# Weights of a hybrid decoder trunk loaded in pairs of chunks: 1 MB transfers into a ring of three pairs

## The chip, the core and the metric

The kernel runs on one core of one Trainium2 chip. The metric is device time in microseconds of one execution, median over runs. TensorE (PE in the profile) multiplies, VectorE is DVE, ScalarE is ACT, GpSimd is POOL, and SyncE (SP) does nothing but issue DMA transfers, in order: an issue that waits for a semaphore holds up all issues behind it. The transfers themselves run on 16 DMA engines that all queues share.

## The reference

A batch of 256 tokens of width 2048 goes through two residual layers, all in float32. Cut to what matters:

```python
h = h + even_layer(h, ...)      # layer 0
h = h + odd_layer(h, ...)       # layer 1

def even_layer(h, ...):
    p = rms_norm(h, norm_g) @ w_in          # 2048 x 9232
    # q, k, v: short conv, silu, l2_norm; beta, decay -> gated DeltaNet, 8 heads of 128, chunks of 64
    #   per chunk: solve (I + A) [u, w] = rhs, A strictly lower triangular, then a scan over 4 chunks
    # glu -> depthwise conv of 31 taps -> layer_norm -> silu
    # q_m -> softmax attention into 256 memory tokens, 4 heads of 256
    return concatenate([o_a, o_b, o_m]) @ w_out    # 3072 x 2048

def odd_layer(h, ...):
    p = rms_norm(h, norm_g) @ w_in          # 2048 x 10240
    # stick-breaking attention, 16 heads of 128; memory attention
    return concatenate([o_c, o_m]) @ w_out         # 3072 x 2048
```

The memory tokens are projected once, by a matrix of 2048 x 2048. All weights together are some 230 MB, each read once.

## The kernel before

**Chunks.** Every projection is cut into jobs of 512 columns, and a job into chunks of 256 rows x 512 columns: 512 KB of float32 each, 432 chunks (0 to 431). A job has 8 chunks, those of the output matrices 4. In each chunk TensorE multiplies two k tiles in three products each, of high parts and remainders: `xhi*whi`, `xhi*wlo`, `xlo*whi` (lines 1671 to 1679). With whole jobs that is 12 products of 512 columns or 24 of 256.

**The way of a chunk c.** SyncE loads it into slot `c % 6` of the ring `raw` (`load_chunk`, L725; `RAWS` is 6). ScalarE rounds it into `whi` (`split`, L927), when the chunk has landed and slot `c % 7` of the second ring is free, that is when TensorE is through with chunk c-7. VectorE computes the remainder `wlo = raw - whi` (`rest`, L1284) and counts `s_lo`; with that the `raw` slot is free. The load of chunk c waits for the remainder of chunk c-6. TensorE takes the chunk when its remainder is made (`do_chunk`).

**The order.** `make_plan` writes one list of steps by position (about one position per chunk), and each engine runs its own steps of it in that order. `split(c)` and `rest(c)` stand up to four positions ahead of TensorE's chunk c, and loads 9 ahead. Between the chunks stand all the other steps: DeltaNet, convolution, norms, attention.

**The start.** Chunks 0 to 7 are loaded by lines of their own (`FIRST` is 8), between pieces of x; loads from the plan begin with chunk 8. In the same stretch x is transposed piece by piece: TensorE (L1723), ScalarE (L973) and VectorE (L1330, `xlo`) each do a part, two pieces for each chunk of the first job.

**The block inversion.** For each of two groups g of four DeltaNet heads the triangular matrices are inverted, from 16x16 diagonal blocks up. The blocks go through DRAM, by four transfers in SyncE's queue, which stand at places that the plan gives among the loads:

- inA (L753, `dn_matrices<-hid`, 512 KB) when VectorE has scaled the four matrices;
- inB (L757, `mix<-dn_matrices`, 64 KB) when inA has landed. VectorE then inverts the blocks (`do_inF`, L1441 to L1447, 29 small instructions in a row);
- inC (L765, `dn_block_inverses<-mix`, 64 KB) when that is done;
- inD (L772, `mix<-dn_block_inverses`, 512 KB) when inC has landed. VectorE then turns the matrices (`do_inT`, L1435, two instructions), and after the first TensorE begins the next level (`do_d4x`, L1831).

Of the kernel before, what the change touches and what calls it, by code (L numbers as in the profile page):

```python
# [52 lines left out]
JOBS = []  # L53
# [32 lines left out]
CH0 = []  # L86
# [6 lines left out]
JOB_OF = [j for j in range(len(JOBS)) for _ in range(JOBS[j][3] // 2)]  # L93
# [35 lines left out]
RAWS, RING, AHEAD = 6, 7, 4  # L129
FIRST = 8  # L130
# [189 lines left out]
def prog(nc, x, mem, vecs, w, a_log, dt_bias, out, last_job=len(JOBS)):  # L320
# [4 lines left out]
    with ctx:  # L325
        def sb(name, shape, dt=F32):
            return ctx.enter_context(nc.sbuf_tensor(name, shape, dt))

        def sem(name):
            return ctx.enter_context(nc.semaphore(name))  # L330


        raw = sb("raw", [128, RAWS, 2, 512])
# [106 lines left out]
        s_raw = [sem(f"raw_chunk_loaded{i}") for i in range(RAWS)]  # L440
# [4 lines left out]
        s_lo = sem("chunk_remainders")  # L445
# [272 lines left out]
        def _(sp):  # L718
            def load_chunk(c):
# [3 lines left out]
                if c >= RAWS:  # L723
                    sp.wait_ge(s_lo, c - RAWS + 1)
                sp.dma_start(raw[:, c % RAWS, :, :], w[name][r:r + 256, c0:c0 + 512].rearrange("(k p) n -> p k n", p=128)  # L725
                             ).then_inc(s_raw[c % RAWS], 16)

            sp.dma_start(*vecs(vrow)[0]).then_inc(s_gain, 16)
            for k, loaded in ((0, s_raw0), (1, s_raw[0])):
                sp.dma_start(raw[:, 0, k, :], w["ev_in"][128 * k:128 * k + 128, JOBS[0][2]:JOBS[0][2] + 512]).then_inc(loaded, 16)  # L730
            for step in (("chunk", 1), ("x", 2), ("chunk", 2), ("x", 3), ("chunk", 3), ("chunk", 4), ("x", 4), ("chunk", 5)):
                if step[0] == "chunk":
                    load_chunk(step[1])
                else:
                    c0, c1 = X_PIECES[step[1]]
# [35 lines left out]
                    sp.wait_ge(s_t[1], LEVELS + 1)  # L771
                sp.dma_start(tinv8, rows_t).then_inc(s_inD, 16)  # L772

            steps = {"load": load_chunk, "inZ": do_inZ, "inA": do_inA, "inB": do_inB, "inC": do_inC, "inD": do_inD}
            for st, i in plan:
                if st in steps:
                    steps[st](i)
# [1 line left out]
            for b in range(4):  # L779
                j = last_job - 4 + b  # L780
# [14 lines left out]
        def _(gp):  # L795
# [87 lines left out]
            def do_sbk(_):  # L883
                gp.wait_ge(s_xl, F_H)
                link(nc.gpsimd.memset(mflat[:, 21 * S:24 * S], 1.0))
                keep(beyond[:, 0:128], [[-1, 128]], -1, 1, ALU.is_gt, 0.0)
                keep(beyond[:, 128:384], [[-1, 256]], 127, 1, ALU.is_gt, 0.0)
                keep(valid[:, 0:128], [[1, 128]], 0, -1, ALU.is_gt, 0.0)
                nc.gpsimd.affine_select(out=valid[:, 256:384], in_=valid[:, 256:384], compare_op=ALU.is_gt, fill=0.0,
                                        base=0, pattern=[[1, 128]], channel_multiplier=-1).then_inc(s_sbk, 1)  # L890
# [17 lines left out]
        def _(sc):  # L908
# [7 lines left out]
            def split(c):  # L916

                if c == 0:
                    sc.wait_ge(s_raw0, 16)
                    act(whi[:, 0, 0, :], raw[:, 0, 0, :], ACT.Copy).then_inc(s_hi0, 1)  # L920
                    return
                sc.wait_ge(s_raw[c % RAWS], 16 * (c // RAWS + 1))
                if c >= RING:
                    sc.wait_ge(s_pe, c - RING + 1)
                if c == 2 * RING - 1:
                    sc.wait_ge(s_bap, 1)
                act(whi[:, c % RING, :, :], raw[:, c % RAWS, :, :], ACT.Copy).then_inc(s_hi, 1)  # L927

            def do_half(_):
                sc.wait_ge(s_raw[0], 16)  # L930
                act(whi[:, 0, 1, :], raw[:, 0, 1, :], ACT.Copy).then_inc(s_hi, 1)

            def do_first(_):
                sc.wait_ge(s_vp, 1)
                act(vt[:, 0:16], M[0][:, 0:16], ACT.Copy).then_inc(s_vt, 1)
                sc.wait_ge(s_vt, 1)
# [310 lines left out]
            def do_xload(b):  # L1247
                sc.wait_ge(s_mixa, 8)
                sc.dma_start(hid[:, :, 512 * b:512 * b + 512],
                             x[:, 512 * b:512 * b + 512].rearrange("(t p) d -> p t d", p=128)).then_inc(s_xre, 16)  # L1250

            steps = {"split": split, "evac": do_evac, "xt": do_xt, "mf": do_mf, "rstd": do_rstd,
                     "rrow": do_rrow, "baw": do_baw, "ba": do_ba, "bat": do_bat,
                     "za": do_za, "dnC": do_dnC, "dnS": do_dnS, "dnB": do_dnB, "dnV": do_dnV, "dnG": do_dnG, "d4x": do_d4x,
# [5 lines left out]
            for b in range(2):  # L1260
                c0, c1 = X_PIECES[b]
# [782 lines left out]
```

## Time and profile before

| | before |
|---|---|
| timed runs, us | 1359.11 median of 3 (1358.84 to 1359.45) |
| the profiled execution, us | 1357.89 |
| its span, us | 1356.2 |
| PE busy | 1347.3 us, 99% |
| DVE busy | 891.5 us, 66% |
| ACT busy | 759.4 us, 56% |
| DMA moved | 239.31 MB, mean 176 GB/s |
| loads of chunks | 431 issues of 512 KB, 4.2 to 4.8 us median to landing |

How to read it: the span is the profiled stretch of one execution, and times below are microseconds from its start. Busy time of TensorE is of pipelined products whose ends are modelled. A timeline row has the start, the length, the engine, the line, the operation, out<-in, the shapes and the count of like instructions merged; in brackets stands how long the engine had been idle before it, and what ended that. SPq rows are issues by SyncE's queue: a merged row lasts from its first issue to the end of its last. Such a row doesn't tell when a transfer landed; that stands in the rows of DMA issues, which have the KB each and the median time from issue to landing.

### The profile page before, as it was taken

What the parts mean: (1) busy time and instruction counts of PE and PEld (TensorE: products, weight loads), DVE (VectorE), ACT (ScalarE), POOL (GpSimd) and SP (SyncE); (2) the same over time, 40 slices, a digit from 0 to 9 for tenths busy, and PEclk for the clock granted to TensorE, in tenths of its full rate; (3) what the DMA queues carried; (4) which work ended last, traced back from release to release, by engine and by line L of the source; (5) the groups of instructions that cost most, each with busy time, mean ns of one, the idle gap of its engine ahead of it and who ended that gap; (6) DMA issues with size and microseconds to landing.
All of it is one profiled execution on the core that took longest, in us unless ns stands there. A gap on an engine that the chain in (4) does not pass through costs nothing.

```text
span 1356.2 us, 18328 instructions
## 1 busy us (share of the span) xinstructions
PE 1347.3 (99%) x6925; PEld 1143.4 (84%) x6925; DVE 891.5 (66%) x1337; ACT 759.4 (56%) x1226; POOL 103.4 (8%) x104
## 2 busy tenths in 40 slices
PE   9999999999999999999999999999999999999998
PEld 8998899888888888888888888888888888888887
DVE  5567688899998987645656455655745736556663
ACT  6556634485355567664445546746757657765341
POOL 2000300003100000000002020020100200000000
PEclk9999999999999999999999999999999999999999
DMA  9665554565646755654556564464464654544662
GB/s 315 194 187 170 154 178 139 156 193 148 192 140 202 269 180 172 203 171 140 171 162 197 185 201 131 165 217 156 161 203 134 202 171 154 189 155 139 201 188 77
DMA packets 134512, 239.31 MB, mean 176 GB/s; under 512 B 13936, under 2 KB 19993, under 8 KB 134425
## 3 DMA queue, kind: packets, MB, share of 16 engines
q1 hardware_dynamic: 131705, 233.43, 54.6%
q10 hardware_dynamic: 2720, 4.72, 1.0%
q8 instruction: 55, 0.90, 0.3%
q14 instruction: 32, 0.26, 0.1%
HBM read 234.32 MB, written 3.80 MB: 176 GB/s over the span
## 4 chain that ended last, share of the span: by engine, by line
PE 77%; DVE 3%; issue 0%; POOL 0%; ACT 0%; DVEq 0%; POOLq 0%
PE job L1671 23%; PE job L1673 23%; PE job L1672 23%; PE mixer L1723 3%; DVE cvr L1533 1%; DVE wlo L1284 1%; PE mixer L1939 1%; PE mixer L1959 1%; PE mixer L1977 1%; PE mixer L1990 1%; PE mixer L1831 0%; PE mixer L1976 0%; PE mixer L1991 0%; PE mixer L1812 0%; DVE hid L1509 0%
## 5 line engine op out<-in xcount | busy, mean ns | idle before, releaser
L1284 DVE TENSOR_TENSOR wlo<-raw,whi 128x1024 fp32r<-128x1024 f32 x431 | 529.1, 1249 | 145.6 <-ACT whi L927 145.5
L1671 PE MATMUL job<-whi,xhi 128*128 128x512 f32 x1536 | 615.3, 401 | 0.0
L1673 PE MATMUL job<-whi,xlo 128*128 128x512 f32 x1536 | 600.0, 391 | 0.0
L1672 PE MATMUL job<-wlo,xhi 128*128 128x512 f32 x1536 | 598.3, 390 | 0.0
L927 ACT ACTIVATE whi<-raw 128x1024 fp32r<-128x1024 f32 x431 | 445.6, 1056 | 158.3 <-PE job L1673 114.8
L1673 PEld LDWEIGHTS job<-whi,xlo 128*128 128x128 f32 x1536 | 288.3, 188 | 62.2
L1672 PEld LDWEIGHTS job<-wlo,xhi 128*128 128x128 f32 x1536 | 289.1, 188 | 55.6
L1671 PEld LDWEIGHTS job<-whi,xhi 128*128 128x128 f32 x1536 | 288.7, 188 | 55.2
L1677 PE MATMUL job<-xhi,whi 128*128 128x256 f32 x376 | 108.3, 288 | 0.7 <-DVE wlo L1284 0.7
L1679 PE MATMUL job<-xhi,wlo 128*128 128x256 f32 x376 | 106.4, 283 | 0.0
L1678 PE MATMUL job<-xlo,whi 128*128 128x256 f32 x376 | 106.3, 283 | 0.0
L1533 DVE SCALAR_TENSOR_TENSOR cvr<-cvr,vt 128x255 f32<-128x255 f32 (+14 forms) x240 | 106.0, 498 | 0.2
L1677 PEld LDWEIGHTS job<-xhi,whi 128*128 128x128 f32 x376 | 72.1, 192 | 0.9 <-issue 0.9
L1678 PEld LDWEIGHTS job<-xlo,whi 128*128 128x128 f32 x376 | 72.1, 192 | 0.0
L1679 PEld LDWEIGHTS job<-xhi,wlo 128*128 128x128 f32 x376 | 72.0, 191 | 0.0
L963 ACT ACTIVATE proj<-job,rstd 128x512 f32<-128x512 f32 x68 | 43.0, 688 | 44.6 <-PE job L1673 40.9
L1316 DVE TENSOR_TENSOR hid<-hid,job 128x512 f32<-128x512 f32 x46 | 29.5, 682 | 42.4 <-PE job L1673 42.4
L1630 DVE SCALAR_TENSOR_TENSOR scr<-mixer,scr 128x384 f32<-128x384 f32 x16 | 8.9, 558 | 60.9 <-ACT scr L1235 60.9
L1233 ACT ACTIVATE scr<-mixer 128x384 f32<-128x384 f32 x16 | 7.9, 492 | 60.0 <-PE mixer L1977 60.0
L832 POOL TENSOR_TENSOR ex<-ei,mhalf 128x16 f32<-128x16 f32 x4 | 15.2, 3808 | 305.0 <-DVE ei L1624 305.0
L973 ACT ACTIVATE xhi<-mixer,vt 128x256 fp32r<-128x256 f32 x48 | 20.8, 470 | 29.7 <-PE mixer L1723 29.7
L1723 PE MATMUL mixer<-ident,proj 128*128 128x128 f32 x208 | 35.5, 272 | 1.1 <-DVE mix L1573 0.6
(278 smaller groups left out, 1004.1 us busy)
## 6 DMA issues: line engine op xcount, KB each, us to landing
raw<-in_od_w_in_dram SPq DMA_DIRECT2D x160, 512.0 KB, 4.4
raw<-in_ev_w_in_dram SPq DMA_DIRECT2D x143, 512.0 KB, 4.2
raw<-in_ev_w_out_dram SPq DMA_DIRECT2D x48, 512.0 KB, 4.8
raw<-in_od_w_out_dram SPq DMA_DIRECT2D x48, 512.0 KB, 4.7
raw<-in_w_mem_kv_dram SPq DMA_DIRECT2D x32, 512.0 KB, 4.5
reg<-in_mem_dram ACTq DMA_DIRECT2D x4, 512.0 KB, 5.0
hid<-in_x_dram ACTq DMA_DIRECT2D x4, 512.0 KB, 8.3
hid<-in_x_dram SPq DMA_DIRECT2D x3, 512.0 KB, 8.6
```

The source lines that it names most:

```text
L927: act(whi[:, c % RING, :, :], raw[:, c % RAWS, :, :], ACT.Copy).then_inc(s_hi, 1)
L963: ins = act(dst, pj[j % 2][t][:, :], ACT.Copy, scale=rstd[:, src, t:t + 1])
L1284: vec.tensor_tensor(wlo[:, c % RING, :, :], raw[:, c % RAWS, :, :], whi[:, c % RING, :, :].bitcast(F32), ALU.subtract).then_inc(s_lo, 1)
L1316: ins = vec.tensor_tensor(v, v, pj[j % 2][t][:, :], ALU.add)
L1533: ins = vec.scalar_tensor_tensor(out=c[:, d:], in0=gsrc[:, 0:S - d], scalar=vt[:, col:col + 1], in1=c[:, d:], op0=ALU.mult, op1=ALU.add)
L1671: mm(out_, xh, hi, start=first, stop=False)
L1672: mm(out_, xh, lo, start=False, stop=False)
L1673: return mm(out_, xl, hi, start=False, stop=last)
L1677: mm(out_, hi[:, cols], xhi[:, k, :], start=first and n % 2 == 0, stop=False, skip_group_check=True)
L1678: mm(out_, hi[:, cols], xlo[:, k, :], start=False, stop=False, skip_group_check=True)
L1679: return mm(out_, lo[:, cols], xhi[:, k, :], start=False, stop=last, skip_group_check=True)
L1723: return nc.tensor.transpose(dst, src, ident[:, :])
```

## The change

From chunk 8 on, SyncE loads two chunks, c and c+1 with c even, in one transfer of 1 MB into two neighbouring slots of `raw`. The ring is the same memory, now three pairs. The transfer waits until the remainders of both chunks that held the two slots are made (c-6 and c-5), and it counts on the semaphore of the even slot. ScalarE waits for that one semaphore for either chunk. The step of the odd chunk in the plan issues nothing. Chunks 0 to 7 are loaded as before. The space in `raw`, the bytes and the run of 2 KB from each row of the weights are the same.

```diff
+            def load_pair(c):
+                if c % 2:
+                    return
+                j = JOB_OF[c]
+                name, r0, c0, _, _ = JOBS[j]
+                r = r0 + 256 * (c - CH0[j])
+                sp.wait_ge(s_lo, c + 2 - RAWS)
+                sp.dma_start(raw[:, c % RAWS:c % RAWS + 2, :, :],
+                             w[name][r:r + 512, c0:c0 + 512].rearrange("(a k p) n -> p a k n", p=128, k=2)
+                             ).then_inc(s_raw[c % RAWS], 16)
...
-            steps = {"load": load_chunk, "inZ": do_inZ, "inA": do_inA, "inB": do_inB, "inC": do_inC, "inD": do_inD}
+            steps = {"load": load_pair, "inZ": do_inZ, "inA": do_inA, "inB": do_inB, "inC": do_inC, "inD": do_inD}
...
-                sc.wait_ge(s_raw[c % RAWS], 16 * (c // RAWS + 1))
+                first = c if c < FIRST else c - c % 2
+                sc.wait_ge(s_raw[first % RAWS], 16 * (first // RAWS + 1))
```

The orders of TensorE, VectorE, ScalarE and GpSimd are the same before and after, only lines below the new function are numbered 11 or 12 higher. SyncE's differs. Its queue at the first group's inversion, before: the 37 loads are those of chunks 20 to 56, the three are 57 to 59, the two 60 and 61. `dn_matrices<-hid` is inA, and the next three without `raw` are inB, inC and inD; in brackets are the semaphores that an issue waits for, `chunk_remainders` being `s_lo`.

```order
L725 DMA raw<-in_ev_w_in_dram 128x2x512 [waits chunk_remainders] x37
L753 DMA dn_matrices<-hid 128x8x128 [waits dn_matrices]
L757 DMA mix<-dn_matrices 64x16x16 [waits inv_matrices_stored]
L725 DMA raw<-in_ev_w_in_dram 128x2x512 [waits chunk_remainders] x3
L765 DMA dn_block_inverses<-mix 64x16x16 [waits inv_scratch_cleared,inv_diagonal_blocks_inverted]
L725 DMA raw<-in_ev_w_in_dram 128x2x512 [waits chunk_remainders] x2
L772 DMA mix<-dn_block_inverses 128x8x128 [waits inv_block_inverses_stored]
```

The same place in SyncE's queue now: the 19 loads are the pairs from 20, 21 to 56, 57.

```order
L735 DMA raw<-in_ev_w_in_dram 128x4x512 [waits chunk_remainders] x19
L764 DMA dn_matrices<-hid 128x8x128 [waits dn_matrices]
L768 DMA mix<-dn_matrices 64x16x16 [waits inv_matrices_stored]
L735 DMA raw<-in_ev_w_in_dram 128x4x512 [waits chunk_remainders]
L776 DMA dn_block_inverses<-mix 64x16x16 [waits inv_scratch_cleared,inv_diagonal_blocks_inverted]
L735 DMA raw<-in_ev_w_in_dram 128x4x512 [waits chunk_remainders]
L783 DMA mix<-dn_block_inverses 128x8x128 [waits inv_block_inverses_stored]
```

Chunk 57's load has moved from behind inB to ahead of inA, together with its wait. SyncE's queue at the second group's inversion, before: loads 62 to 107, inA, inB, loads 108 to 110, inC, loads 111 and 112, inD.

```order
L725 DMA raw<-in_ev_w_in_dram 128x2x512 [waits chunk_remainders] x46
L753 DMA dn_matrices<-hid 128x8x128 [waits dn_matrices]
L757 DMA mix<-dn_matrices 64x16x16 [waits inv_matrices_stored]
L725 DMA raw<-in_ev_w_in_dram 128x2x512 [waits chunk_remainders] x3
L765 DMA dn_block_inverses<-mix 64x16x16 [waits inv_block_inverses_loaded,inv_diagonal_blocks_inverted]
L725 DMA raw<-in_ev_w_in_dram 128x2x512 [waits chunk_remainders] x2
L772 DMA mix<-dn_block_inverses 128x8x128 [waits inv_updated1,inv_updated0,inv_block_inverses_stored]
```

And now: pairs up to 106, 107; two pairs, 108, 109 and 110, 111, ahead of inC; pair 112, 113 ahead of inD.

```order
L735 DMA raw<-in_ev_w_in_dram 128x4x512 [waits chunk_remainders] x23
L764 DMA dn_matrices<-hid 128x8x128 [waits dn_matrices]
L768 DMA mix<-dn_matrices 64x16x16 [waits inv_matrices_stored]
L735 DMA raw<-in_ev_w_in_dram 128x4x512 [waits chunk_remainders] x2
L776 DMA dn_block_inverses<-mix 64x16x16 [waits inv_block_inverses_loaded,inv_diagonal_blocks_inverted]
L735 DMA raw<-in_ev_w_in_dram 128x4x512 [waits chunk_remainders]
L783 DMA mix<-dn_block_inverses 128x8x128 [waits inv_updated1,inv_updated0,inv_block_inverses_stored]
```

Chunk 111's load has moved ahead of inC, and chunk 113's ahead of inD.

## Rows read from the trace of the kernel before

**Rows 1.** The page: busy time by engine, and TensorE's granted clock in tenths.

```profile
PE 1347.3 (99%) x6925; PEld 1143.4 (84%) x6925; DVE 891.5 (66%) x1337; ACT 759.4 (56%) x1226; POOL 103.4 (8%) x104
...
PEclk9999999999999999999999999999999999999999
```

**Rows 2.** TensorE's waits: for whom, us in total, times, longest us.

```profile
PE mixer L1723 <- DVE mix L1573: 0.6, 1, 0.6
PE mixer L1723 <- ACT scr L1125: 0.6, 1, 0.6
...
PE mixer L1831 <- POOL reg L862: 0.4, 1, 0.4
```

**Rows 3.** Timeline of the second layer, VectorE from 879 and ScalarE from 883.

```profile
879.57 10.32 DVE L1284 TENSOR_TENSOR wlo<-raw,whi 128x1024 fp32r<-128x1024 f32 x6
...
889.58 0.47 ACT L1225 ACTIVATE cvr<-mixer,qgain 128x256 f32<-128x256 f32 x1 [4.76 <-PE mixer L1723]
```

**Rows 4.** DMA issues at 16.20 (load 8), 22.4 (load 9), 157.1 (56), 163.6 (inB).

```profile
raw<-in_ev_w_in_dram SPq DMA_DIRECT2D x1, 512.0 KB, 9.5
...
raw<-in_ev_w_in_dram SPq DMA_DIRECT2D x1, 512.0 KB, 4.6
...
raw<-in_ev_w_in_dram SPq DMA_DIRECT2D x1, 512.0 KB, 3.7
...
mix<-dn_matrices SPq DMA_DIRECT2D x1, 64.0 KB, 2.9
```

**Rows 5.** Timeline from 16 to 30: SyncE, ScalarE, VectorE, TensorE.

```profile
16.20 6.64 SPq L725 DMA_DIRECT2D raw<-in_ev_w_in_dram  x2
...
25.72 1.06 ACT L927 ACTIVATE whi<-raw 128x1024 fp32r<-128x1024 f32 x1 [1.68 <-DMA raw<-in_ev_w_in_dram]
...
27.96 0.87 DVE L1330 SCALAR_TENSOR_TENSOR xlo<-mixer,vt,xhi 128x256 fp32r<-128x256 f32 x2
...
29.20 0.36 PE L1677 MATMUL job<-xhi,whi 128*128 128x256 f32 x1
```

**Rows 6.** Timeline of SyncE's queue, 160 to 191: inA, inB, inC, inD.

```profile
160.43 0.37 SPq L753 DMA_DIRECT2D dn_matrices<-hid  x1
163.62 0.69 SPq L757 DMA_DIRECT2D mix<-dn_matrices  x1
...
176.05 0.60 SPq L765 DMA_DIRECT2D dn_block_inverses<-mix  x1
...
179.87 0.47 SPq L772 DMA_DIRECT2D mix<-dn_block_inverses  x1
```

**Rows 7.** Timeline of VectorE and TensorE, 162 to 180: remainders, the inversion's first step.

```profile
162.73 1.21 DVE L1284 TENSOR_TENSOR wlo<-raw,whi 128x1024 fp32r<-128x1024 f32 x1
...
169.28 0.16 DVE L1441 TENSOR_SCALAR mix<-mix 64x15 f32<-64x15 f32 x1
...
177.08 1.21 DVE L1284 TENSOR_TENSOR wlo<-raw,whi 128x1024 fp32r<-128x1024 f32 x1
...
179.13 0.28 PE L1677 MATMUL job<-xhi,whi 128*128 128x256 f32 x1
```

**Rows 8.** Timeline at 187: VectorE turns the first matrix, TensorE's next level.

```profile
186.77 0.71 DVE L1435 STREAM_TRANSPOSE mix<-mix 128x512 f32<-128x512 f32 x1 [2.80 <-DMA mix<-dn_block_inverses]
...
187.77 1.06 PE L1831 MATMUL mixer<-mix,reg 128*128 128x128 f32 x8
```

**Rows 9.** Timeline of the second group: inC, inD, VectorE's turn, TensorE's next level.

```profile
347.08 0.59 SPq L765 DMA_DIRECT2D dn_block_inverses<-mix  x1
...
349.82 0.40 SPq L772 DMA_DIRECT2D mix<-dn_block_inverses  x1
...
356.78 0.71 DVE L1435 STREAM_TRANSPOSE mix<-mix 128x512 f32<-128x512 f32 x1 [1.44 <-DMA mix<-dn_block_inverses]
...
357.59 1.13 PE L1831 MATMUL mixer<-mix,reg 128*128 128x128 f32 x8
```

**Rows 10.** Busy time by engine, with granted clock, DMA share and GB/s, 165 to 180.

```profile
165.00:180.00 15.00, 15.00 (x128) 15.00 (x127) 14.04 (x41) 6.63 (x7) 0.00 (x0) 1.00 0.49 122
```

## The prediction

> **What bounds the kernel now.** Read the page first. TensorE is busy 99% of the span, and its granted clock is full in all 40 slices [rows 1]. So only time in which TensorE waits can be won, and every microsecond in which it is made to wait is lost. Next come TensorE's own waits: after the start the longest are 0.6, 0.6 and 0.4 us in total, and none of these is ended by a weight load [rows 2]. The loads are hidden: ScalarE makes a chunk's high part and VectorE its remainder well before TensorE reaches it. What matters is therefore the few places where TensorE starts within a few tenths of a microsecond of the step that it needs, and where that step hangs on SyncE's queue. The timeline has three: chunk 6, while the ring fills, and the two DeltaNet groups' block inversions, whose four transfers inA to inD stand in the same queue as the loads.
>
> **What the change does, part by part.** From chunk 8 on, 424 issues become 212. SyncE's time is on no path by itself, and no byte is saved: nothing gained. The order on the other engines stays. Three things move. (1) A pair c, c+1 waits for the remainder of chunk c-5, where load c waited for c-6. (2) Both halves count as landed when the second is. (3) Chunk c+1's load, with its wait, now stands at chunk c's place in the queue, ahead of whatever lay between.
>
> Where no inversion is near, (1) and (2) cost nothing. The tightest spot in the second layer comes once in each of four head groups. There a run of six remainders begins on VectorE at 879.57; the pair 284, 285 waits for the first of them, until 880.8 [rows 3]. A lone load takes 3.7 us from issue, and a second half 1.3 more (below) [rows 4]: it lands near 885.8. ScalarE had finished chunk 284 at 884.8 (889.58 less its idle 4.76) [rows 3], so it would finish near 886.9, about 2 us late, and still be idle 2.7 us before TensorE gives it the next step. I take 0.
>
> **Start.** Loads 8 and 9 are issued from 16.20, the second from about 22.4 to 22.84 [rows 5]; they land 9.5 us after 16.20 and 4.6 after 22.4 [rows 4], at 25.7 and 27.0. The DMA engines are full here, so the pair lands at 27.0. ScalarE had been idle until chunk 8 landed (25.72); behind that chunk, in its order and VectorE's, stand the last pieces of x for chunk 6. VectorE ends them at 27.96 + 0.87 = 28.83, and TensorE begins chunk 6 at 29.20 [rows 5]: 0.4 us of room. Cost 1.3 - 0.4 = 0.9. Bounds: 0 (ScalarE catches up) and 1.7.
>
> **First inversion.** Pair 56, 57 stands ahead of inA, as the order above shows, and waits for the remainder of chunk 51, made by 162.73 + 1.21 = 163.94 [rows 7]. Load 57, which waited for it before, stood behind inB. So inA, issued at 160.43, goes out at 163.95 + 0.37 = 164.3: 3.9 us later. It also queues behind 1 MB. The pair lands 3.7 + 1.3 us after its issue, near 169.0. inA landed 3.2 us after its issue with no fresh load ahead (160.43 to 163.62, where inB, that waits for it, is issued) [rows 6]. Behind the pair I give its half megabyte 1.5 us, a little over a load's 1.3, since it moves in shorter pieces: 170.5. inB lands 2.9 us after its issue [rows 4]: 173.4. VectorE began the inversion at 169.28 without waiting [rows 7]; now it waits until 173.4, 4.1 us. Behind it stands the remainder of chunk 54, 177.08 to 178.29, which TensorE takes at 179.13 [rows 7]. With 0.8 of room TensorE stands still for 3.3 us. inC follows the inversion (176.05) and moves by 4.1. Pair 60, 61 waits for the second remainder behind the inversion, as load 61 did, and so inD (179.87) moves by 4.1 too [rows 6]. Half of the bytes ahead of inD start up to 1.1 us later than before, of which I take 0.1, since inD was waiting for bytes and not for its issue. VectorE had already waited 2.80 us for inD, and has turned the first matrix at 186.77 + 0.71 = 187.48; TensorE takes it at 187.77 [rows 8]. With 0.3 of room the group costs 4.2 - 0.3 = 3.9 us in all, the 3.3 within it. Lower bound: if the pair doesn't hold inA up, inA lands at 164.3 + 3.2, inB at 170.4, VectorE waits 1.1, and TensorE 0.8. Upper: 3.9 + 1.1 = 5.0.
>
> **Second inversion.** Here inA keeps its place in time, but pair 110, 111 stands ahead of inC, where only load 110 did. It waits for the remainder of chunk 105, the first behind the inversion on VectorE; load 111 waited for that one behind inC. VectorE's inversion let inC go at 347.08 [rows 9]; one remainder of 1.2 us and one issue later it goes out at 348.6, 1.5 later. It stands behind 1 MB issued at 348.2, which lands near 353.2, and so lands itself near 354, in place of at most 349.8. inD, issued at 349.82, goes out near 354.2, with pair 112, 113 ahead of it. Between inC's old place and inD there are now 2 MB, in place of 1 MB (loads 111 and 112): at 1.3 us for half a megabyte 2.6 us more, if the DMA engines had no idle time before. They had some: inD landed 7.0 us after its issue (356.78), though 1.5 MB take only 3.9. I take 1.7 of the 2.6. The room is 357.59 - (356.78 + 0.71) = 0.1 [rows 9]. Cost 1.7 - 0.1 = 1.6; bounds 0.9 (inC not held up by the pair) and 4.5 (inD takes its 7.0 us from the later issue).
>
> **Given back.** TensorE's waits of 0.6, 0.6 and 0.4 [rows 2] shrink where TensorE comes late and the other engine doesn't. I take 1.0 of the 1.6; bounds 0.5 and 1.6.
>
> **Sum.** 0.9 + 3.9 + 1.6 - 1.0 = 5.4 us. The profiled execution took 1357.89 (span 1356.2), so one like it would take 1363.3. The median of the timed runs is 1359.11, and I put the change on that: **1364.5 us**. Bounds of the terms together: 0 + 0.8 + 0.9 - 1.6 = 0.1 and 1.7 + 5.0 + 4.5 - 0.5 = 10.7.
>
> **A rule that speaks for the change.** Loads 8 and 9 land 1.3 us apart [rows 4, 5]: in a burst, half a megabyte per 1.3 us, 400 GB/s. By these rows a larger transfer isn't faster in a full queue. The Trainium skill ("DMA: Bandwidth & Descriptors", section "Bandwidth") advises at least 1 MiB for each transfer, and measured 6.15 us for 1 MB issued from GpSimd. By the page's 6.15 in place of my 5.0 the pair ahead of inA would land 1.1 us later, and the sum would be 6.5. The trace has no transfer of 1 MB.
>
> **Rivals.** *No slower.* A transfer of the inversion isn't held up by a pair ahead of it: the engines serve both at once. Then the first group costs 0.8 and the second 0.9; with 0.4 at the start and 1.0 given back the sum is 1.1: 1360.2. It decides at one point, whether inA lands by 168 or after 170. Against it: inD took 7 us with two loads ahead, inA 3.2 with none [rows 6, 8]. For it: nothing in the trace stands behind 1 MB.
> *Faster.* The pairs empty the queue sooner, and inD lands earlier. Its room is what TensorE waits on this chain, the 0.4 us of L1831 [rows 2]: 1358.7.
> *The clock.* No row shows a granted clock below full, and none a long stop of TensorE after the start [rows 1, 2]. My forecast puts stops of 3.3 and 1.6 us there. If the clock fell to 1.2 GHz after such a stop, the chunk behind it, 24 products at 15.00/128 = 0.12 us [rows 10], would take 5.8 us in place of 2.9. Once or twice that is 1367.4 or 1370.3. The Trainium skill ("TensorE: Matmul & The Clock Gate", section "Why this matters for your kernels") warns of idle gaps between bursts of matmuls that bring the lower clock back; no run here shows it yet.
> *Slower elsewhere.* ScalarE's delays of the second layer reach TensorE in the four head groups, by up to 1 us each: 1368.5.
>
> **How the numbers follow.** Forecast 0.60, no slower 0.19, faster 0.02, clock 0.11, slower elsewhere 0.08. A measurement of this kernel tells about 0.2%, 2.7 us, from no change. The forecast, the clock and the last rival lie beyond that, but for a low tail of 0.02 of the forecast: slower 0.77. Same is 0.19 + 0.02 = 0.21. Faster by over 0.2% has no mechanism of that size; I leave it the 0.02. The range, 1360.0 to 1369.5, takes in the first rival, nearly all of the bounds (1359.2 to 1369.8) and one chunk at half clock; less than 0.2 is left out.
>
> **What would show it.** In the timeline of the changed kernel: inA issued near 164.3 plus the shift of the start, and landing over 6 us later; VectorE idle for some 4 us before the first instruction of the inversion, released by the transfer that fills the blocks; TensorE waiting about 3.3 us near 180 for a remainder; inC of the second group right behind a pair; chunk 6 late by 1 us. If VectorE doesn't wait before the first inversion, the largest term is wrong. If ScalarE's waits for loads reach TensorE elsewhere, I have misread how well (1) and (2) are hidden.

## The result, and the profile after

| | before | changed |
|---|---|---|
| timed in the same rounds, us | 1358.97 median of 4 (1358.84 to 1359.45) | 1368.64 median of 4 (1368.04 to 1369.14) |
| the profiled execution's span, us | 1356.2 | 1366.3 |

The ratio is 1.0071, with a 95% interval of 1.0059 to 1.0083: 9.7 us slower, where 5.4 were forecast. The time lies within the range, near its upper end. By the time alone the rivals *the clock* (1367.4) and *slower elsewhere* (1368.5) stand nearer to it than the forecast; the profile and the experiments have to tell them apart.

The page of the changed kernel, busy time by engine and granted clock, answers to [rows 1]; behind them stand the loads' issues with the KB of each and the median time to landing.

```profile
PE 1349.8 (99%) x6925; PEld 1145.3 (84%) x6925; DVE 892.2 (65%) x1337; ACT 759.2 (56%) x1226; POOL 102.4 (7%) x104
...
PEclk9999999999999999999999999999999999999999
...
raw<-in_od_w_in_dram SPq DMA_DIRECT2D x80, 1024.0 KB, 5.2
raw<-in_ev_w_in_dram SPq DMA_DIRECT2D x68, 1024.0 KB, 5.1
```

The page alone would not find the loss: its shares and its row of tenths read as before. TensorE's waits, in answer to [rows 2], do (for whom, us in total, times, longest us):

```profile
PE job L1689 <- DVE wlo L1296: 5.9, 2, 5.3
PE mixer L1843 <- issue: 1.7, 1, 1.7
...
PE mixer L1735 <- DVE xlo L1342: 1.1, 1, 1.1
PE mixer L1735 <- DVE mix L1585: 0.6, 1, 0.6
PE mixer L1735 <- ACT scr L1137: 0.6, 1, 0.6
...
PE mixer L1843 <- POOL reg L873: 0.4, 1, 0.4
```

Three new stops, 5.3, 1.7 and 1.1 us, and the three small ones of before unchanged. Set against each other product by product, TensorE of the changed kernel runs 1.2 us late from 29 us on, 6.6 from the first inversion's stop, 8.5 at 190, 10.1 from the second inversion to the end. The difference of the spans is 10.1.

**Start** (timeline, in answer to [rows 5]).

```profile
27.01 1.06 ACT L939 ACTIVATE whi<-raw 128x1024 fp32r<-128x1024 f32 x1 [3.03 <-DMA raw<-in_ev_w_in_dram]
...
29.24 0.87 DVE L1342 SCALAR_TENSOR_TENSOR xlo<-mixer,vt,xhi 128x256 fp32r<-128x256 f32 x2
...
29.87 0.41 PE L1735 MATMUL mixer<-ident,hid 128*128 128x128 f32 x2 [1.09 <-DVE xlo L1342]
...
30.42 0.36 PE L1689 MATMUL job<-xhi,whi 128*128 128x256 f32 x1
```

The pair lands at 27.0, as forecast. The row of `xlo` begins 1.28 us later than before and TensorE's chunk 6 1.22 us later (30.42 against 29.20).

**First inversion.** SyncE's queue, in answer to [rows 6]: the pair 56, 57, inA, inB, a pair, inC, a pair, inD.

```profile
165.15 0.37 SPq L735 DMA_DIRECT2D raw<-in_ev_w_in_dram  x1
165.56 0.51 SPq L764 DMA_DIRECT2D dn_matrices<-hid  x1
173.86 0.69 SPq L768 DMA_DIRECT2D mix<-dn_matrices  x1
174.59 0.65 SPq L735 DMA_DIRECT2D raw<-in_ev_w_in_dram  x1
183.43 0.60 SPq L776 DMA_DIRECT2D dn_block_inverses<-mix  x1
186.84 0.38 SPq L735 DMA_DIRECT2D raw<-in_ev_w_in_dram  x1
187.26 0.51 SPq L783 DMA_DIRECT2D mix<-dn_block_inverses  x1
```

The DMA issues between 165.1 and 165.9 with their time to landing, to be read beside [rows 4]:

```profile
raw<-in_ev_w_in_dram SPq DMA_DIRECT2D x1, 1024.0 KB, 5.9
dn_matrices<-hid SPq DMA_DIRECT2D x1, 512.0 KB, 8.3
```

How the end of inA's 8.3 us was spent stands in the DMA view of three stretches, 171.60 to 172.17, 172.17 to 172.57 and 172.57 to 173.40. The columns of the queue rows are the packets that began, MB, and the share of the 16 engines' time:

```profile
q1 hardware_dynamic: 114, 0.05, 32.0%
q8 instruction: 1, 0.02, 10.3%
...
DMA packets 0, 0.00 MB, mean 0 GB/s; under 512 B 0, under 2 KB 0, under 8 KB 0
...
q1 hardware_dynamic: 20, 0.01, 7.4%
```

Of inA's more than 1000 packets all but the last 20 had begun by 172.2, 1.2 us behind the pair's landing at 171.0. Then nothing began for 0.4 us, and the last 20 dripped out until 173.4. A single packet of 16 KB, of the queue that the profile calls instruction, was under way meanwhile: it began near 171.66 and took 0.94 us (10.3% of 16 engines in 0.57 us), so it ended at 172.6, where the last 20 begin. That it stood on the DMA engine which still had these 20 to move is argued from the times; the profile doesn't say which engine a packet took.

VectorE and TensorE of the same stretch, in answer to [rows 7, 8]: inversion, remainders, the first product of chunk 54, the turned matrices.

```profile
176.67 0.17 DVE L1453 TENSOR_SCALAR mix<-mix 64x15 f32<-64x15 f32 x1 [6.13 <-DMA mix<-dn_matrices]
...
184.47 6.89 DVE L1296 TENSOR_TENSOR wlo<-raw,whi 128x1024 fp32r<-128x1024 f32 x6
...
185.73 0.58 PE L1689 MATMUL job<-xhi,whi 128*128 128x256 f32 x1 [5.26 <-DVE wlo L1296]
...
193.67 1.30 DVE L1447 STREAM_TRANSPOSE mix<-mix 128x512 f32<-128x512 f32 x2 [2.32 <-DMA mix<-dn_block_inverses]
```

inA, which before took 3.2 us, takes 8.3; VectorE waits 6.13 us for inB's blocks, and TensorE 5.26 for the remainder behind them. Then the clock. Busy time in three stretches; the column behind POOL's is the granted clock, 1.00 in [rows 10]:

```profile
180.00:183.00 3.00, 0.47 (x4) 0.27 (x3) 2.59 (x13) 2.00 (x2) 0.00 (x0) 1.00 0.00 0
...
183.00:187.00 4.00, 1.27 (x6) 1.27 (x7) 3.93 (x7) 0.00 (x0) 0.00 (x0) 0.50 0.14 16
...
190.00:195.00 5.00, 5.00 (x44) 5.00 (x43) 2.68 (x5) 2.01 (x2) 0.00 (x0) 1.00 1.08 361
```

From 183.0, while TensorE stood still, until 189.8 the granted clock is half, 1.2 GHz. The products from 185.73 on run at that: 1.9 us more.

**Second inversion**, in answer to [rows 9]: inC and inD in SyncE's queue, VectorE's turn, TensorE's next level.

```profile
357.17 0.59 SPq L776 DMA_DIRECT2D dn_block_inverses<-mix  x1
...
362.63 0.37 SPq L783 DMA_DIRECT2D mix<-dn_block_inverses  x1
...
366.88 1.30 DVE L1447 STREAM_TRANSPOSE mix<-mix 128x512 f32<-128x512 f32 x2 [2.63 <-DMA mix<-dn_block_inverses]
...
367.69 1.13 PE L1843 MATMUL mixer<-mix,reg 128*128 128x128 f32 x8 [1.71 <-issue]
```

TensorE's level comes 10.1 us after that of before, 1.6 of it new. The profile puts the 1.71 us of waiting down to issue, that is to nothing that it shows; that the level waits for the turned matrix is read from the order of the steps and from the times (the turn begins at 366.88, the level at 367.69).

### The profile page after: what moved, and what is told of

Read it like the earlier page. It is cut to its first block, busy times and chain, and to the rows that moved or that the text cites. A ratio compares the mean times of both kernels' runs of the same rounds, so it can differ in the third digit from the quotient of the medians.

```text
span 1366.3 us, 18116 instructions
## 1 busy us (share of the span) xinstructions
PE 1349.8 (99%) x6925; PEld 1145.3 (84%) x6925; DVE 892.2 (65%) x1337; ACT 759.2 (56%) x1226; POOL 102.4 (7%) x104
## 4 chain that ended last, share of the span: by engine, by line
PE 76%; DVE 3%; issue 1%; POOL 0%; ACT 0%; DVEq 0%; POOLq 0%
PE job L1683 23%; PE job L1685 23%; PE job L1684 23%; PE mixer L1735 3%; DVE cvr L1545 1%; DVE wlo L1296 1%; PE mixer L1951 1%; PE mixer L1971 1%; PE mixer L1989 1%; PE mixer L2002 1%; PE mixer L1843 0%; PE mixer L1988 0%; PE mixer L2003 0%; PE mixer L1824 0%; DVE hid L1521 0%
## 5 line engine op out<-in xcount | busy, mean ns | idle before, releaser
L1735 PE MATMUL mixer<-ident,proj 128*128 128x128 f32 x208 | 35.5, 272 | 1.2 <-DVE mix L1585 0.6
```

Of the source, the lines that this page charges most:

```text
L1735: return nc.tensor.transpose(dst, src, ident[:, :])
```

## The experiments

The theory after the result: the time is lost in SyncE's queue, where a load with its wait, and its bytes, stand ahead of the inversions' transfers; the size of the transfer has no part in it, and the half clock follows from the stop. Rivals: the 1 MB transfer itself is slow to land; the pairs cost elsewhere too; the clock falls on its own. Each kernel below was timed in five rounds beside the kernel before, whose median was 1358.6 to 1359.1 us throughout. In the diffs `...` stands for lines left out.

### The pair at the later chunk's place

```diff
             def load_pair(c):
-                if c % 2:
+                if c % 2 == 0:
                     return
+                c -= c % 2
```

> Pairs of 1 MB as in the changed kernel, but issued at the odd chunk's place in SyncE's queue instead of the even one's: pair 56, 57 then stands behind inB, and pair 110, 111 behind inC, as loads 57 and 111 did before. My theory: of the 9.7 us, 5.3 (TensorE's wait at the first inversion), 1.9 (the half clock behind it) and 1.6 (second inversion) come from the place of the pairs in the queue, so that they vanish and only the 1.2 us of the start stay: about 1360.2 us, with TensorE's longest wait after the start under 0.7. Rival, that the size of the transfers or the later slot release is what costs, wherever the pairs stand: 1366 to 1369.

Measured: 1359.08 us, ratio 1.0006 (0.9997 to 1.0015), 1.1 us less than the theory had. The same 212 transfers of 1 MB with the same waits, issued one place later, cost nothing that can be told. SyncE's queue of this kernel at the first inversion, inA, inB, the pair, inC:

```profile
161.57 0.37 SPq L765 DMA_DIRECT2D dn_matrices<-hid  x1
164.78 0.68 SPq L769 DMA_DIRECT2D mix<-dn_matrices  x1
165.51 5.38 SPq L736 DMA_DIRECT2D raw<-in_ev_w_in_dram  x2
177.19 0.60 SPq L777 DMA_DIRECT2D dn_block_inverses<-mix  x1
```

inA lands 3.2 us after its issue again, and everything is 1.1 late by the start alone. At the second inversion inD, with half a megabyte less ahead of inC, landed 5.8 us after its issue, where it took 7.0 before. Of this 0.3 to 0.4 us reach TensorE, which is 1.1 us late ahead of it and 0.8 behind it, and 0.7 at the end. The granted clock stays full.

### Two transfers of 512 KB at the pair's place

Against the kernel before; ScalarE waits for each chunk's own semaphore, as there.

```diff
+            def load_pair(c):
+                if c % 2:
+                    return
+                sp.wait_ge(s_lo, c + 2 - RAWS)
+                for c in (c, c + 1):
...
+                    sp.dma_start(raw[:, c % RAWS, :, :], w[name][r:r + 256, c0:c0 + 512].rearrange("(k p) n -> p k n", p=128)
+                                 ).then_inc(s_raw[c % RAWS], 16)
```

> Two transfers of 512 KB with semaphores of their own in place of each 1 MB transfer, issued one behind the other at the pair's place and behind the pair's wait. My theory (place and wait cost, size doesn't): SyncE still holds inA until the remainder of chunk 51, and inA still stands behind 1 MB: the waits at both inversions and the half clock stay, only the start's 1.2 us shrinks, since chunk 8 counts as landed by itself: about 1367.5. Rival, that one transfer of 1 MB is slower or blocks the queue more than two of 512 KB: inA lands 6 us or less after its issue instead of 8.3, TensorE's wait falls to about 3 and the clock stays: 1363 to 1364.

Measured: 1367.61 us, 1.0067 (1.0055 to 1.008). inA lands 7.2 us after its issue, VectorE waits 5.77, TensorE 4.9. The stop at the start is gone, since chunk 8 counts as landed by itself, and the half clock was 3.4 us long in place of 6.8. Beside the pairs of 1 MB without the stop at the start (*The start*, below: 1367.56 us) the halves are equal, so place and wait cost the time, and the size nothing that the medians tell. In the profiled executions inA did land sooner behind two halves, 7.2 us after its issue and 8.2 after that of the first half, against 8.3 and 8.7 behind 1 MB.

### Only pair 56, 57 at the later place

```diff
-                if c % 2:
+                if c % 2 != (c in (56, 57)):
                     return
+                c -= c % 2
```

> The changed kernel with one pair alone, 56 and 57, moved to the odd chunk's place, behind inB; every other pair as it is. My theory: inA goes out when VectorE has made its input, the wait of 5.3 us and the half clock of 6.8 us behind it go (7.2 us), the start (1.2) and the second inversion (1.6) stay: about 1361.6. Rival, that the DMA engines' load of 1 MB pieces delays inA to inD wherever the pair stands: TensorE's wait near 180 stays over 2 us, 1364 or more.

Measured: 1361.02 us, 1.0019 (1.001 to 1.0028). One transfer of 212, moved by one place, takes back 7.6 us of the 9.7: the first inversion's stop and the half clock behind it. TensorE is 1.1 late from the start and 1.4 more from the second inversion. Together with the start this is the whole of the rest.

### Load 57 alone ahead of inA

The kernel before, with single loads, and one of them moved.

```diff
             for st, i in plan:
+                if (st, i) == ("load", 57):
+                    continue
                 if st in steps:
                     steps[st](i)
+                if (st, i) == ("load", 56):
+                    load_chunk(57)
```

> The kernel before with one edit: the single load of chunk 57 (512 KB, its own wait for the remainder of chunk 51) moved from behind inB to ahead of inA. No pairs. My theory: SyncE holds inA back until 164.3 again, 3.9 us late; it stands behind 512 KB instead of 1 MB, so it lands some 5 us after its issue instead of 8.3, near 169.5, and VectorE waits about 3 us; TensorE loses 2.5 to 3: about 1361.3, too short a stop for half the clock to be sure. Rival, that the loss of the change needs the 1 MB: under 1359.5.

Measured: 1362.5 us, 1.0026 (1.0015 to 1.0036). inA is issued at 164.45 and lands 5.3 us later; VectorE waits 3.16, TensorE 2.3. The stretch behind that stop, with its clock of 0.50:

```profile
182.80:186.00 3.20, 3.20 (x17) 3.20 (x16) 3.20 (x3) 0.59 (x1) 0.00 (x0) 0.50 0.93 287
```

The half clock makes TensorE 1.6 us later still; the expectation had left it out, and the time is 1.2 over it. So the wait moves inA by 4.0 us whatever the transfer, and what goes out behind that wait adds the rest: inA landed after 3.2 us with no fresh load ahead, 5.3 with 512 KB, 7.2 to 8.3 with 1 MB.

### The start

```diff
             def load_pair(c):
+                if c < 16:
+                    return load_chunk(c)
...
-                first = c if c < FIRST else c - c % 2
+                first = c if c < 16 else c - c % 2
```

> The changed kernel, but chunks 8 to 15 still loaded one at a time, pairs from chunk 16. My theory: chunk 8 lands by itself near 25.7, TensorE's wait of 1.1 us for the x pieces of chunk 6 goes, the two inversions stay: 1.2 us less than the changed kernel, about 1367.4. Rival: the start's delay is made up later anyway (TensorE waits at the inversion for VectorE, which waits for SyncE), so that it comes back as a longer wait near 180: 1368.6, same.

Measured: 1367.56 us (1366.64 to 1370.28), 1.0068 (1.0055 to 1.008). The stop at the start is gone, and the time lies 1.1 us under the changed kernel's. The profiled execution, 1370.28, had a second half clock, of 3.4 us at 368, behind a stop of 2.2. That the start is worth its 1.2 us is shown by the stop that is gone from the profile; the times agree, but they spread over more than that.

### Both

Pairs at the later place, and single loads up to chunk 15.

```diff
             def load_pair(c):
-                if c % 2:
+                if c < 16:
+                    return load_chunk(c)
+                if c % 2 == 0:
                     return
+                c -= c % 2
...
-                first = c if c < FIRST else c - c % 2
+                first = c if c < 16 else c - c % 2
```

> Pairs at the odd chunk's place and chunks 8 to 15 one at a time: both repairs together. My theory: nothing of the loss is left, and the 0.4 us that the kernel with pairs at the odd place won at the second inversion stays: 1358.2, against 1358.6 before. Rival, that pairs have a cost of their own beside place and start: 1359.5 or more.

Measured: 1357.94 us, 0.9992 (0.9984 to 1.0001). All that the change costs is taken back, and 208 fewer issues win nothing that a measurement can tell.

### Products in the stop, to hold the clock

The changed kernel with 24 products of the identity by itself, into a bank of sums that is free then, ahead of chunk 54's wait; they take part in no result.

```diff
+                if c == 54:
+                    pe.wait_ge(*evac_done(j - 1))
+                    for _ in range(24):
+                        mm(pj[(j + 1) % 2][0][:, 0:128], ident[:, :], ident[:, :], start=True, stop=True)
                 pe.wait_ge(s_lo, c + 1)
```

> The changed kernel with 24 products of the identity (128 columns each) ahead of TensorE's wait for the remainder of chunk 54, written to a PSUM bank that is free there: TensorE works through most of the wait. My theory: the half clock that is granted from 183.0 for 6.8 us comes from the stop of 5.3 us; with the stop filled the granted clock stays full there and 1.9 us come back: about 1366.8, with the remainder of chunk 54 at the same time. Rival, that the clock falls for another reason or the loss is made up behind it (the next level waits for inD anyway): 1368.6, same.

Measured: 1369.1 us (1366.57 to 1369.77), 1.0073 (1.006 to 1.0086), where 1366.8 were expected. The five runs fall into two groups: 1366.57 and 1367.36 with a mean granted clock of 1.000, and 1369.1 to 1369.77 with 0.999. In the profiled one, of the second group, the half clock is gone from the first stop and stands behind one of 2.5 us at the second inversion. The same for both stops, with nine more such products ahead of the second inversion's level:

```diff
+                if i == 14 + BASE:
+                    take("d4x", i)
+                    for _ in range(9):
+                        mm(M[0][:, 0:128], ident[:, :], ident[:, :], start=True, stop=True)
                 pe.wait_ge(s_of[par], inv_level(i) + 1)
```

> The changed kernel with both long stops of TensorE filled with products of the identity: 24 ahead of chunk 54 as before, and 9 ahead of the first level of the second inversion. My theory: the half clock follows the stops, wherever one is left (with only the first filled it came at the second in three of five runs); with both filled the clock stays full in every run and all runs lie near 1366.8, none over 1367.5. Rival, that the clock falls whatever TensorE does in the stops: some runs still near 1369.

Measured: 1367.96 us (1366.96 to 1368.41), 1.0066 (1.0053 to 1.008). Half of what was expected held. The clock follows the stops: with the first filled, the granted clock of 183 to 187 is 1.00, and with both filled the mean clock of all five runs is 1.000, and in the profiled one it is full up to the last microseconds. The two busy rows are of the first and of the second kernel:

```profile
183.00:187.00 4.00, 3.74 (x33) 3.55 (x32) 3.93 (x7) 0.00 (x0) 0.00 (x0) 1.00 0.16 20
369.00:372.00 3.00, 3.00 (x8) 2.32 (x8) 2.77 (x6) 1.28 (x2) 0.00 (x0) 0.50 0.56 148
```

```profile
183.00:187.00 4.00, 3.90 (x34) 3.71 (x33) 3.93 (x6) 0.00 (x0) 0.00 (x0) 1.00 0.16 20
367.00:371.00 4.00, 3.49 (x20) 3.07 (x20) 4.00 (x8) 1.54 (x2) 0.00 (x0) 1.00 0.59 178
```

But the time didn't fall by the 1.9 us; it fell by 0.7, which the two intervals don't tell from nothing, and four of the five runs lie over the 1367.5 that none was to pass. The gain was given back behind it. VectorE of the second kernel at the second inversion:

```profile
348.54 0.17 DVE L1453 TENSOR_SCALAR mix<-mix 64x15 f32<-64x15 f32 x1 [1.23 <-DMA mix<-dn_matrices]
```

inA was issued at 337.74 in place of 339.32, but landed at 345.74 in place of 345.79, 8.0 us after its issue; so the inversion can't begin earlier, and VectorE now waits for it. Why inA lands at the same time, though it and the pair ahead of it go out 1.6 us sooner, can be read from the DMA view in part. The two rows are of this kernel from 344.18 to 345.50, and of the changed kernel from 344.2 to 345.5:

```profile
q1 hardware_dynamic: 52, 0.03, 6.6%
...
q1 hardware_dynamic: 659, 0.33, 84.2%
```

In this kernel all but 52 of inA's packets had begun by 344.2, 1.1 us and more ahead of the changed kernel's. The last 52 came one behind another at 6.6% of the 16 engines, which is about what one engine moves. Here too a packet of 16 KB of the instruction queue lies among inA's, at 342.6, and the changed kernel has none there. That it held this one engine back is argued, and that the two landings then agree to 0.05 us is chance as far as the runs show.

### The wait alone

The kernel before, with single loads in their old places, each of which waits for one remainder more, as the pairs do.

```diff
                 if c >= RAWS:
-                    sp.wait_ge(s_lo, c - RAWS + 1)
+                    sp.wait_ge(s_lo, c - RAWS + (1 if c < FIRST else 2))
```

> The kernel before, single loads of 512 KB at their own places, but from chunk 8 on each waits for the remainder of chunk c-5 instead of c-6: the later release alone. My theory (a wait in SyncE's queue ahead of a transfer of the inversion is what costs, however it gets there): load 56 now waits until 163.9 ahead of inA, inA goes out near 164.3 behind 512 KB, VectorE waits about 3 us; load 110 waits for the first remainder behind the second inversion ahead of inC, 1.5 us, for about 1 us more: 1362. Rival, that only moving a load in the queue costs and the hiding of the later release holds everywhere: 1358.6, same.

Measured: 1368.74 us (1366.91 to 1370.64), 1.0075 (1.0062 to 1.0089). The expectation was off by almost 7 us: no load has another place or size, and the loss is as large as that of the whole change. That the two totals agree is chance, for they are made up otherwise. At the first inversion TensorE loses 4.4 us here, a half clock of 3.4 us included, against 7.3 in the changed kernel. At the second it loses 4.6 against 1.6, with a second half clock: load 107, which stands ahead of that group's inA and in a pair waits for nothing more than before, here waits for the remainder of chunk 102, and inA goes out 4.8 us after its place.

```profile
339.89 0.48 SPq L753 DMA_DIRECT2D dn_matrices<-hid  x1
```

Two more runs cut the waits in two. First all but those of the six loads that stand directly ahead of inA, inC and inD:

```diff
+                    sp.wait_ge(s_lo, c - RAWS + (1 if c < 16 or c in (56, 59, 61, 107, 110, 112) else 2))
```

> The kernel before with its single loads, but from chunk 16 on each load waits for the remainder of the chunk five before it in place of six; the loads of chunks 56, 59, 61, 107, 110 and 112, which stand directly ahead of the inversions' transfers in SyncE's queue, keep the old wait. Theory, that a later wait costs only where such a transfer stands behind it: the time of the kernel before, 1358.9 us, the granted clock at full speed, and no wait of TensorE for VectorE of over 2 us. Rival, that the later release also costs between the inversions: 1361 us or more. If the loads one place further ahead delay the transfers as well, VectorE's wait at 172 us is over 1 us.

Measured: 1360.3 us, 1.0012 (1.0003 to 1.0021), between the theory and its rival. Then those six alone:

```diff
+                    sp.wait_ge(s_lo, c - RAWS + (2 if c in (56, 59, 61, 107, 110, 112) else 1))
```

> The kernel before with its single loads, in which only the loads of chunks 56, 59, 61, 107, 110 and 112, which stand directly ahead of the inversions' transfers in SyncE's queue, wait for the remainder of the chunk five before them in place of six. It is the counterpart of the run in which these six alone kept the old wait (1360.3, where all together cost 1368.7). Theory, that the cost lies in these six waits: 8 to 10 us over the kernel before, 1367 to 1369 us; in the trace VectorE waits some 3 us at 172 and at 348, TensorE over 2 us behind each, with a half clock behind them. Rival, that it takes all loads of a group together (the loads behind, too, are released later): 1364 us or less. If only the first inversion shows it, 1363 to 1365 us.

Measured: 1368.41 us (1367.68 to 1369.63), 1.0072 (1.0058 to 1.0085). TensorE's waits in this kernel:

```profile
PE job L1677 <- DVE wlo L1284: 2.9, 2, 2.2
PE mixer L1831 <- issue: 2.5, 2, 2.0
PE job L1671 <- DVE wlo L1284: 2.3, 1, 2.3
```

The theory of 1367 to 1369 held, though only the second of the two stops has a half clock behind it. VectorE before either inversion:

```profile
172.94 0.17 DVE L1441 TENSOR_SCALAR mix<-mix 64x15 f32<-64x15 f32 x1 [3.10 <-DMA mix<-dn_matrices]
...
348.95 0.17 DVE L1441 TENSOR_SCALAR mix<-mix 64x15 f32<-64x15 f32 x1 [3.30 <-DMA mix<-dn_matrices]
```

In the kernel with single loads six waits of over 400 cost 9.3 us, and all the others together, from chunk 16 on, 1.5; all at once cost 9.9, so the two don't quite add up. The 1.5 lies at the inversions as well: in the profiled execution TensorE is 1.2 us late from the first group's level on and 2.4 from the second's. In the first inD was issued at 180.46 in place of 179.87, behind load 60, which was let go later and which the list of six had left out, and took 7.6 us to land. So "directly ahead" was drawn too narrowly; every load of the stretch counts.

### Pairs behind both inversions only

```diff
             def load_pair(c):
+                if c < 114:
+                    return load_chunk(c)
                 if c % 2:
                     return
...
-                first = c if c < FIRST else c - c % 2
+                first = c if c < 114 else c - c % 2
```

> The kernel before with single loads up to chunk 113, and pairs of 1 MB at the earlier chunk's place from chunk 114 on, behind both inversions. Theory, that pairs neither cost nor win anything where no other transfer stands behind them: the time of the kernel before, 1358.9 us. Rival, that pairs delay the second layer elsewhere too: 1360 us or more. Rival, that fewer transfers save time: under 1358 us.

Measured: 1358.66 us, 1.0001 (0.9992 to 1.0009). 159 pairs at the earlier chunk's place, with their later wait, change nothing in the rest of the first layer or in the second, where the working had taken 0 for the delays at [rows 3].

## Why the prediction was right, and where it was off

**Where the time goes: right.** All three places were named, with the engine that waits and what it waits for, and no fourth exists: in the trace of the changed kernel TensorE's delay grows nowhere else, and the last run excludes the rival *slower elsewhere*, whose 1368.5 the time alone would have borne out. The first two runs exclude the transfer's size as the cause. *Faster* and *no slower* fell with inA, which landed at 173.8, the latter by its own test (by 168, or after 170).

**Start: 0.9 forecast, 1.2 measured.** The 1.3 us by which the pair lands later was right. The 0.4 of room was not there: between `xlo` and chunk 6 stand two transposes of TensorE (the L1735 row at 29.87), which wait for `xlo` themselves and so move with it.

**First inversion: 3.9 forecast, 5.4 measured.** This is the mis-sized term, and it lies above its own upper bound of 5.0. inA's issue was right: 164.3 plus the 1.2 of the start is 165.5, measured 165.56. inB's 2.9 was 2.8. The step that failed is inA's landing, 6.2 us after its issue by the sum, 8.3 measured. The pair took 5.9 and not 5.0, and inA's half megabyte landed 2.8 us behind it (171.0 to 173.8), not 1.5. The length of its pieces isn't the reason: all but 20 of its packets had begun 1.2 us behind the pair's landing, and without these 20 inA would have landed some 1.6 us behind it (an estimate: 172.2 and the 0.5 us that its landing came behind its last packet). The last 20 packets took 1.2 us more, and no term of the sum stood for that. The two make the 2.1 us that were missing, 0.9 and 1.2, and they go straight into VectorE's wait (6.1 for 4.1) and TensorE's (5.3 for 3.3). The 1 MB loads' median is 5.0 to 5.2 us, as forecast from the trace. The pairs with inA right behind them took more: 5.9 here, 5.8 at the second inversion, and 5.9 in the kernel of *The start*. The Trainium skill ("DMA: Bandwidth & Descriptors", section "Bandwidth") has 6.15 us for 1 MB, which comes nearer to the 5.9 here. But that is the time in which the DMA engines were busy with a transfer issued from GpSimd, not the time from an issue by SyncE to landing, so the nearness is luck. The larger size won nothing here (1357.94 us against 1358.73, ratio 0.9984 to 1.0001, with place and start repaired).

The group's other 0.6, for inD, did not come, since the half clock had made TensorE later still. In the kernel with both stops filled, where the clock is full, TensorE's delay does grow at this level, from 6.6 to 6.9 us, so half of the term was there.

**The clock: 0 in the sum, 1.9 measured.** The rival with a chance of 0.11 and 2.9 us a stop came true beside the forecast, once in the profiled execution. The reason given for it was right: a stop that no row of before had. Its chance was low, as the runs show now, for the changed kernel and six of the experiments have stops of TensorE of over 2 us, and each shows a half clock behind one of them at least. Its size was too high, because the half clock began within the stop and covered only 4.1 us of products, not a whole chunk. The Trainium skill ("TensorE: Matmul & The Clock Gate", section "Why this matters for your kernels") warns of this for idle gaps between bursts; the trace agrees, with 183.0 to 189.8 at 0.5.

**Second inversion: 1.6 forecast, 1.6 measured.** inC went out 1.6 later than the shift so far and landed 5.4 us after its issue; inD was issued at 362.63, 354.1 without the shift of 8.5, forecast 354.2.

**Given back: 1.0 forecast, 0 measured.** The waits of 0.6, 0.6 and 0.4 are all still there. They were taken to shrink where TensorE comes late and the other engine doesn't, so the other engines came late by as much; that this is because TensorE's own products feed them is argued.

**Sum.** 1.2 + 5.4 + 1.9 + 1.6 = 10.1, the difference of the spans; by the medians it is 9.7. The forecast missed it by 0.3 + 1.5 + 1.9 + 1.0 = 4.7 us, every miss to the same side, so none made up for another. The place and the way of the loss were foreseen; its size was only within a wide range.

**One sentence was wrong, and the bounds hid it.** The working said of the later wait (1) that it costs nothing where no inversion is near, which holds. Near one, it laid the first inversion's loss on chunk 57's move. The last experiments show that the wait is enough without any move: load 56, in its old place, waiting for the remainder of chunk 51, holds inA up by as much (it goes out at 164.28, forecast 164.3 for the pair). The move and the wait are two ways to the same wait ahead of the same transfer.

## What to carry to other kernels

In a queue that issues in order, a load's wait is also the wait of everything behind it: before loads are merged or a ring's release is changed, list the short transfers that an engine is waiting for, and look at every wait and every byte in the queue ahead of each. A merged load belongs at the place of its later part, where its wait is due anyway; there it was free but for the start (1359.08 us against 1358.59). At the place of its earlier part it cost 9.7 us, and with single loads six later waits of over 400 made 9.3 of 9.9. And where the loads are hidden, fewer and larger transfers win nothing.

## What the runs showed of the hardware

- A 512 KB transfer in pieces of 512 bytes, issued 0.4 us behind a load: 3.2 us to landing with no fresh load ahead, 5.1 to 5.3 behind one of 512 KB, 7.2 behind two, 8.3 behind one of 1 MB. In the last two cases the last 18 to 20 packets dripped in behind the others, over 0.7 and 1.2 us, right behind a packet of 16 KB of the instruction queue.
- TensorE's granted clock fell to half for 3.4 us behind stops of 2.2 to 4.9 us, and for 6.8 us behind stops of 5.3 and 5.6 us. The first made TensorE 1.6 to 1.7 us later, the second 1.9 and 2.5. The same stop of 2.2 us left it full in another kernel. TensorE's wait at 182 in the kernel with six later waits, and the clock around it:

```profile
182.02 0.39 PE L1677 MATMUL job<-xhi,whi 128*128 128x256 f32 x1 [2.24 <-DVE wlo L1284]
```

```profile
180.00:184.00 4.00, 1.98 (x16) 1.99 (x17) 4.00 (x4) 0.00 (x0) 0.00 (x0) 1.00 0.21 29
184.00:188.00 4.00, 4.00 (x36) 4.00 (x35) 3.56 (x4) 1.06 (x1) 0.00 (x0) 1.00 1.01 293
```

What decides between the two the runs leave open.
